# Gate and up products of two SwiGLU blocks: one product of 512 columns for high and low activations, a bank per output half

## What is computed

```python
def swiglu(x, w_gate, w_up, w_down):
    return (jax.nn.silu(x @ w_gate) * (x @ w_up)) @ w_down

h = h + 0.5 * swiglu(rms_norm(h, ffn1_norm[i]), ffn1_w_gate[i], ffn1_w_up[i], ffn1_w_down[i])
...   # sparse attention, retention, merge, output projection
h = h + 0.5 * swiglu(rms_norm(h, ffn2_norm[i]), ffn2_w_gate[i], ffn2_w_up[i], ffn2_w_down[i])
gate = jax.nn.sigmoid(rms_norm(h, ple_norm[i]) @ w_ple_gate[i])
h = h + gate * (p[i] @ w_ple_proj[i])
```

## Time and profile before

| | us |
|---|---|
| median of 3 runs | 1147.44 (1146.24 to 1151.64) |
| profiled execution | 1146.73 |
| its span, first to last instruction | 1144.9 |
| PE busy | 1097.3 (96%) |
| DVE busy | 707.1 (62%) |
| ACT busy | 516.7 (45%) |
| TensorE share of the chain that ended last | 73% |

### The profile page before, as it was taken

How to read it: one execution, slowest core, us unless ns; L and a number is a source line. 1 busy time by engine, 2 the same in 40 slices (tenths; PEclk the granted TensorE clock), 3 DMA queues, 4 the chain that set the end, 5 groups by cost and what they waited for, 6 DMA issues and landing times.

```text
span 1144.9 us, 19072 instructions
## 1 busy us (share of the span) xinstructions
PE 1097.3 (96%) x7962; PEld 931.6 (81%) x7962; DVE 707.1 (62%) x1129; ACT 516.7 (45%) x803; POOL 0.2 (0%) x4
## 2 busy tenths in 40 slices
PE   5989999899999999999999989999999999999997
PEld 3789888554555554999999978888799999999996
DVE  2889777322332334785865679986656775655667
ACT  3774224111111113754444477377944554443455
POOL 0000000000000000000000000000000000000000
PEclk9999999899999999999999999999999999999998
DMA  9955618999999947365554433443336545445321
GB/s 384 399 198 212 247 50 324 422 421 415 412 404 410 409 190 318 144 236 198 199 196 158 158 111 129 146 139 103 104 139 228 202 170 218 184 161 208 129 92 38
DMA packets 38155, 257.74 MB, mean 225 GB/s; under 512 B 4368, under 2 KB 5264, under 8 KB 7856
## 3 DMA queue, kind: packets, MB, share of 16 engines
q1 hardware_dynamic: 36720, 252.38, 57.6%
q10 hardware_dynamic: 1344, 4.08, 0.9%
HBM read 255.39 MB, written 1.05 MB: 224 GB/s over the span
## 4 chain that ended last, share of the span: by engine, by line
PE 73%; DVE 15%; ACT 6%; issue 3%; DMA 2%; ACTq 0%; DVEq 0%
PE bank L535 72%; DVE wl L1811 4%; ACT wh L1242 2%; DMA early<-in_w_ada 1%; DMA csts<-in_cst 1%; DVE xt L1861 1%; DVE arena L2397 1%; DVE rstd L1835 1%; DVE small L2396 1%; ACT arena L1252 1%; DVE acc L1873 1%; DVE hl L1878 1%; PE bank L921 0%; ACT arena L1590 0%; ACT L1252 0%
## 5 line engine op out<-in xcount | busy, mean ns | idle before, releaser
L535 PE MATMUL bank<-hh,wh 128*128 128x256 f32 (+2 forms) x1256 | 362.8, 289 | 6.1 <-DVE wl L1811 4.3
L535 PE MATMUL bank<-hl,wh 128*128 128x256 f32 (+2 forms) x1256 | 358.3, 285 | 0.0
L535 PE MATMUL bank<-hh,wl 128*128 128x256 f32 (+2 forms) x1256 | 358.3, 285 | 0.0
L1811 DVE TENSOR_TENSOR wl<-raw,wh 128x1024 fp32r<-128x1024 f32 (+4 forms) x238 | 267.6, 1163 | 82.7 <-ACT wh L1242 79.3
L1242 ACT ACTIVATE wh<-raw 128x1024 fp32r<-128x1024 f32 (+4 forms) x238 | 227.8, 1003 | 70.0 <-PE bank L535 69.9
L535 PEld LDWEIGHTS bank<-hh,wh 128*128 128x128 f32 (+1 forms) x1256 | 240.8, 192 | 15.4 <-issue 10.4
L535 PEld LDWEIGHTS bank<-hl,wh 128*128 128x128 f32 (+1 forms) x1256 | 240.9, 192 | 1.1
L535 PEld LDWEIGHTS bank<-hh,wl 128*128 128x128 f32 (+1 forms) x1256 | 240.9, 192 | 1.0
L535 PE MATMUL bank<-yh,wh 128*128 128x256 f32 x512 | 146.8, 287 | 0.5 <-DVE yl L1831 0.5
L535 PE MATMUL bank<-yl,wh 128*128 128x256 f32 x512 | 145.5, 284 | 0.0
L535 PE MATMUL bank<-yh,wl 128*128 128x256 f32 x512 | 145.5, 284 | 0.0
(11 more groups left out here) (279 smaller groups left out, 1392.8 us busy)
## 6 DMA issues: line engine op xcount, KB each, us to landing
raw<-in_gu SPq DMA_DIRECT2D x40, 1024.0 KB, 11.0
arena<-in_gu SPq DMA_DIRECT2D x24, 1024.0 KB, 9.9
raw<-in_gd SPq DMA_DIRECT2D x22, 1024.0 KB, 8.6
raw<-in_w_adt SPq DMA_DIRECT2D x14, 1024.0 KB, 5.6
raw<-in_f1g SPq DMA_DIRECT2D x11, 1024.0 KB, 4.8
raw<-in_f1d SPq DMA_DIRECT2D x11, 1024.0 KB, 5.4
raw<-in_f2g SPq DMA_DIRECT2D x11, 1024.0 KB, 4.8
raw<-in_f2u SPq DMA_DIRECT2D x11, 1024.0 KB, 4.9
```

The costliest lines, as they stand in the source:

```text
L535: return pe.matmul(o, l, m, start=start, stop=stop, skip_group_check=True)
L1811: v.tensor_tensor(WL[slot_of[U]][:, 0:n], src, WH[slot_of[U]][:, 0:n].bitcast(f32), ALU.subtract).then_inc(S("wl"), 1)
```

## The change

- Gate and up weights are laid out anew on the host: a unit is now one output half (128 columns) with all eight input blocks, not both output halves with four input blocks (`halves` in place of `even`).
- `hh` and `hl` become one tensor `hb`, so that high and low activations of one input block can be named as one operand of 2 x 256 columns (`HL0`, `HL1`).
- `lin_wide` replaces `lin_fm` for the gate and up products of f1 and f2: for each output half and input block one product of 512 columns with the high weights (high and low activations side by side in a bank) and one of 256 columns with the low weights into the bank's first half. A product takes a bank for each output half. For the very first gate block, whose input arrives block by block, the halves are interleaved by four input blocks.
- VectorE adds the two halves of a bank (`ffn_sum`, a tensor_reduce over pairs of columns 256 apart) into SBUF, for two gate banks and two up banks a step. The scaling and the product with the up part then read SBUF; the order is gate sums, scale, up sums, scale, wait for SiLU, product, low part.
- The bank plan: f1 step 0 has 4, 0 (gate) and 5, 6 (up), step 1 has 1, 2 and 7, 4, later steps 0, 1 and 2, 3. f2 has 0, 1 and 2, 3 in every step, with 4 for the last of step 0.

The core of the diff:

```diff
-            HHt, HLt = ob("hh", 4096), ob("hl", 4096)
+            HB = ob("hb", 8192)
...
+        HHt, HLt = HB[:, 0:4096], HB[:, 4096:8192]
...
+        HB5 = HB[:, :].rearrange("p (s h k t) -> p s h k t", s=2, h=2, k=8)
+        HL0, HL1 = HB5[:, :, 0], HB5[:, :, 1]
...
-        rot = over([0, 1, 2, 3])
-        job(("f1", "g", 0), 4)
-        job(("f1", "u", 0), 5)
+        by_half = lambda P, i, *banks: fixed_to(banks, *[(P, c, i, m) for c in "gu" for m in range(2)])
+        by_half("f1", 0, 4, 0, 5, 6)
         job("f1a", 3)
-        for i in range(1, 11):
-            rot(("f1", "g", i), ("f1", "u", i))
+        by_half("f1", 1, 1, 2, 7, 4)
+        for i in range(2, 11):
+            by_half("f1", i, 0, 1, 2, 3)
...
-        rot = over([0, 1, 2])
         for i in range(11):
-            rot(("f2", "g", i), ("f2", "u", i))
+            by_half("f2", i, 0, 1, 2, 3 if i else 4)
...
+            def lin_wide(P, c, i, X, ready=None):
+                U = 2 * where[P + c, i]
+                bs, ws = {}, {}
+                for m, x in [(m, 4 * u + k) for u in range(2) for m in range(2) for k in range(4)] if ready else [(m, x) for m in range(2) for x in range(8)]:
+                    if x == 0:
+                        ws[m] = weights(U + m, 8)
+                        bs[m] = take(pe, (P, c, i, m))
+                    if ready and m == 0:
+                        pe.wait_ge(*nth(ready[0], ready[1][x]))
+                    h, l = ws[m]
+                    mm(two(bs[m]), h[:, x, :], X[:, :, x, :], x == 0, False)
+                    t = mm(bs[m][:, 0:256], l[:, x, :], X[:, 0, x, :], False, x == 7)
+                    if x == 7:
+                        t.then_inc(S("used"), 1)
...
-            def ffn_act(i, P, G, T, rs, g, u):
-                done(v, g, i)
+            def ffn_sum(i, P, c, T, m):
+                v.wait_ge(*nth("used", units_used(2 * where[P + c, i] + m)))
+                b = bank((P, c, i, m))
+                return v.tensor_reduce(T[i % 2][:, m, :].unsqueeze(2), b[:, :].rearrange("p (s t) -> p t s", s=2), AX.X, ALU.add)
+
+            def ffn_gate(i, P, G, rs):
                 if i >= 2:
-                    evicted(v, (P, "u", i - 2))
-                v.tensor_tensor(G[i % 2], two(bank((P, "g", i))), rs, ALU.mult).then_inc(copied((P, "g", i)), 1)
-                v.wait_ge(*nth(P + "_s", i + 1))
-                done(v, u, i)
+                    v.wait_ge(*nth(P + "_t", i - 1))
+                ffn_sum(i, P, "g", G, 0).then_inc(copied((P, "g", i, 0)), 1)
+                step(ffn_sum(i, P, "g", G, 1))
+                evicted(v, (P, "g", i, 0))
+                prev()
+                v.tensor_tensor(G[i % 2], G[i % 2], rs, ALU.mult).then_inc(copied((P, "g", i, 1)), 1)
+
+            def ffn_up(i, P, G, T, rs):
                 if i >= 2:
                     v.wait_ge(*nth(P + "_yl", i - 1))
-                v.tensor_tensor(T[i % 2], G[i % 2], two(bank((P, "u", i))), ALU.mult).then_inc(copied((P, "u", i)), 1)
-                evicted(v, (P, "u", i))
-                v.tensor_tensor(T[i % 2], T[i % 2], rs, ALU.mult).then_inc(S(P + "_t"), 1)
+                for m in range(2):
+                    ffn_sum(i, P, "u", T, m).then_inc(copied((P, "u", i, m)), 1)
+                for m in range(2):
+                    evicted(v, (P, "u", i, m))
+                chain(v.tensor_tensor(T[i % 2], T[i % 2], rs, ALU.mult))
+                v.wait_ge(*nth(P + "_s", i + 1))
+                v.tensor_tensor(T[i % 2], T[i % 2], G[i % 2], ALU.mult).then_inc(S(P + "_t"), 1)
+                v.wait_ge(*nth(P + "_t", i + 1))
                 low_act(i, P, T)
...
+    def halves(w):
+
+        K, n = w.shape
+        return np.ascontiguousarray(w.reshape(K // 128, 128, n // 256, 2, 128).transpose(2, 1, 3, 0, 4).reshape(n // 256, 128, 2 * K))
```

## The result

The changed kernel takes 1160.97 us (median of 4 runs, 1158.88 to 1163.70), the kernel before beside it 1148.76 (4 runs, 1146.24 to 1151.64): a ratio of 1.0102, 95% interval 1.0081 to 1.0124. That is 1.0% slower, in the forecast's direction, but about twice the forecast's size, and 1 us above the range of 1149 to 1160. The profiled execution took 1158.88 us with a span of 1157.1, against 1146.73 and 1144.9.

A forecast was written before the change was run, and what follows sets the result against it. TensorE, 96% busy, was taken as the bound. On 1146.73 us: +9.6 (f1's start), -3.4 (rest of f1), +3.4 (f2's start), -4.3 (rest of f2), +1.6 (clock) = +6.9, so 1153.6 us; range 1149 to 1160.

The forecast's parts named there:

- the banks: Starts of f1 and f2: TensorE waits for banks that VectorE frees late, costing +9.6 us and +3.4 us.
- the sums: VectorE's four added bank sums a step: 0.69 us each, 2.7 us a step, costed at nothing in the steady loop.
- The upper bound of 1.22 us: Most that one VectorE sum of a bank was allowed to take; the lower bound was 0.61 us.
- rival B: VectorE becomes the bound: sums take 1.22 us, 2.1 us more per step, about 1159.5 us in all; chance 12%.
- Cover just holds: f1's step 5: despite VectorE's extra jobs, the gate sum comes 1.9 us before TensorE wants its bank back.
- the clock in f2: After 3.8 us idle in f2, one stretch of some 3.4 us at 1.2 GHz was to cost +1.6 us.
- The bounds of 0 and 3.2 us: Lowest and highest cost allowed for the low clock behind f2's idle stretch, around the expected 1.6 us.
- the saving of a pair: Gate and up products of f1 and f2: one 512- and one 256-column product take 0.347 us, saving 13.3 ns.
- they start 0.22 to 0.23 us apart: Spacing of 512-column products elsewhere in the kernel, taken as 0.227 us, against 0.24 for two of 256.
- Rival A: Wide product saves nothing, its operand being two pieces or the fixed part doubling: 7.7 us missing, 1161 us; chance 12%.
- Step 0's up and step 1's gate save 0.43, so step 1's up starts at 478.66: Start of f1: two faster blocks bring step 1's up product and the statistics product 0.43 us earlier.
- rival D: Bank waits as forecast, but the clock falls more often, twice in f1 or longer in f2: 1155 to 1158; chance 15%.

The follow-up runs named there:

- experiment 1: Changed kernel with steps 0 to 2 of f1 and step 0 of f2 in the old form on old banks: 1144.22 us, ratio 0.9943 to the kernel before.
- experiment 2: Also written narrow_f1: changed kernel with only steps 0 to 2 of f1 in the old form, f2 wide throughout: 1149.28 us, ratio 0.9997.
- experiment 3: Changed kernel with only step 0 of f2 in the old form, f1 wide from step 0: 1159.74 us, ratio 1.0075.
- experiment 12: Changed kernel with the old form at both starts, as in experiment 1, and every sum of a bank made twice: 1151.70 us, ratio 1.0018.
- experiment 10: Changed kernel with small unread products meant to fill TensorE's three idle stretches and keep the clock up: 1164.26 us, ratio 1.0124.
- split_product: Changed kernel with every 512-column product made as two of 256 columns, banks and sums kept: 1164.02 us, ratio 1.0141.
- experiment 5: Changed kernel with high and low activations of an input block stored side by side, so the operand is one piece: 1161.81 us, ratio 1.0116.
- experiment 7: The kernel of experiment 1 with eight 512-column products first, then eight of 256, in each output half: 1141.75 us, ratio 0.9929.
- experiment 11: Also written first_split: changed kernel with only f1's very first gate block making its wide product as two of 256 columns: 1160.75 us, ratio 1.0090.

## Why the prediction was half right

**Right: the banks.** Step 1's up product was to idle 8.2 us and did 7.93; step 2's second gate half was to go on at 498.35 and did at 499.46, with TensorE already 0.95 us behind at the statistics product; f2 was to idle 3.8 and idled 3.50. Statistics product to step 3 was predicted as 478.0 to 518.2, 40.2 us, and was 40.58. Experiments 1, 2 and 3 show that these waits go when the banks are not reused, each at its own place.

**Right: the sums.** 0.69 us taken from the earlier trace rows, 685 ns measured for all 88. The upper bound of 1.22 us and with it rival B are out, although the Trainium skill (VectorE: DVE Perf Modes, "Rules for kernel authors") calls tensor_reduce the slowest operation of the engine: here it equals the tensor_tensor of the same input size. "Cover just holds" was right too: in f1's steps 3 to 10 no wait for a sum, with 21% of VectorE's time left; experiment 12 shows that twice the sums would not have fitted there.

**Right in size, not certain: the clock in f2.** 1.6 us predicted from the earlier trace rows, 1.56 and 1.34 measured by experiments 10 and 2. But with the same 3.50 us of idling the clock was low for 3.4 us in the changed kernel, not at all in narrow_f1, and for 6.8 us in first_split and split_product, where it fell 0.8 and 1.5 us before TensorE went on. First_split's last piece took 177.08 us, 2.6 more than narrow_f1's. The bounds of 0 and 3.2 us hold all of these.

**Wrong in size: the saving of a pair.** The step that failed is "they start 0.22 to 0.23 us apart": I took 0.227 from a stretch of the first block in which products of 512 columns follow each other. In f1 and f2 a wide product is followed by a narrow one after 0.237 us, and a pair saves 6.7 ns instead of 13.3. Over 576 pairs that is 3.8 us that were not given back, 1.7 in f1 and 2.1 in f2; the table's rows for the rest of f1 and of f2 are short by 1.6 and 1.8. Rival A had named the term and was right by half. Its first reason was not: experiment 5 rules out the two-piece operand. Experiment 7 gives half of it to the alternation of sizes, for 0.231 + 0.119 us. The other half stands in the first products of each group; why they are slower stays open. By the Trainium skill (TensorE: Matmul & The Clock Gate, "Back-to-back issue gap") a pair would save 2.5 ns; the measured 6.7 lies between its rule and my row, and nearer to the rule.

**Missed: the wait ahead of step 0's up product.** The second step that failed is "Step 0's up and step 1's gate save 0.43, so step 1's up starts at 478.66": it lets step 0's up product start when it did before, and has the clock at full speed behind it. The up product starts 8.79 us after f1's first product, 8.13 before, and TensorE idles 2.42 us ahead of it instead of 1.64. Behind that the clock fell to 0.50 for 3.4 us. The statistics product came 1.96 us later instead of 0.43 earlier. Of these 2.4 us, 0.66 are the later start (8.79 - 8.13) and 1.7 the clock (1.56) with the half-sized saving of two blocks (0.2).

The faster block alone doesn't make the longer idle stretch: its last product starts just 0.14 us earlier (6.08 against 6.22 us after the first). The rest of the 0.78 us is the later start. What TensorE waits for is not the weight split that the trace names before:

```profile
466.82 0.36 PE L535 MATMUL bank<-hh,wh 128*128 128x256 f32 x1 [1.64 <-DVE wl L1811]
```

That split (465.22 to 466.45) had ended 0.37 us earlier, in the changed kernel 1.25 us earlier. The first gate block is the end of a branch in TensorE's program, and the DMA records show transfers of instructions here. Queue 8 in two stretches of 5 us, 461.7 to 466.7 before and 460.3 to 465.3 after (packets, MB, share of 16 engines):

```profile
q8 instruction: 2, 0.03, 2.9%
```

```profile
q8 instruction: 2, 0.03, 4.3%
```

Queue 8 made 66 of these 16 KB transfers for 7962 products before and 60 for 7258 after, 121 products each, so I take it for TensorE's. The two transfers start 3.79 and 5.18 us after f1's first product before, 4.58 and 5.00 after, and both are over at 6.49 and 7.11. In all fourteen traces TensorE goes on 1.46 to 1.71 us after that: the nine kernels with a narrow first block have the transfers at 6.35 to 6.70, the five with a wide one at 6.98 to 7.43. So the wait fits one for instructions behind the branch, and these came later. Why they come later behind a wide block no run shows.

Experiment 11 shows that the first block sets it off: that block slowed again, nothing else, the low clock gone, 2.2 us back. The other traces agree: in the five kernels with a wide first block the idle stretch here is 2.18 to 2.45 us and the clock falls behind it, in the nine with a narrow one (the kernel before among them) it is 1.51 to 1.82 and it doesn't.

**The sum again.** Predicted +6.9, measured +12.2 in the profiled executions. The 5.3 us between them: start of f1 2.7, rest of f1 1.6, start of f2 0.2, rest of f2 1.8, and -1.0 in the stages that the change doesn't touch.

**The range.** Rival A at 1161 and rival D at 1155 to 1158 were weighed as cases that exclude each other, next to a forecast with each term at its best value. They are terms of one sum: half of A and a low stretch as in D, with the later start ahead of it, came together, 3.8 + 2.4 us, and lead from 1153.6 to 1159.8. A range of independent terms has to take in two of them going wrong the same way. The chances of a slower kernel (0.60) were on the right side, and would have been larger.

## What to carry to other kernels

When an operand takes more banks, list for each bank its last reader's time and its next writer's time at the start of the stage, not in the steady loop, and do it again for the plan that repairs it: here the gain of 3.9 us in 576 pairs was paid back three times over by three waits, 12.8 us, and moving one wait off a bank made a longer one on another. If only the first steps are short of banks, give only these the old form: that turned 1.0% slower into 0.6% faster (0.7% with products of one size in a row). A product made faster ahead of a wait gives nothing; look at what the wait is for, since here it got longer and the clock fell behind it.

## What the hardware showed that I had not expected

- A product's distance to the next depends on its neighbours: 512 columns take 0.227 us in the earlier trace rows and 0.237 in turns with 256 columns; in groups of eight 0.235 to 0.239 for the first two and 0.227 for the last three, even for the very last, which 256 columns follow. 256 columns take 0.116 in turns with wide ones, 0.119 to 0.12 among themselves.
- A moving operand in two pieces 4096 columns apart streams like one in one piece (0.237 and 0.116 us both ways).
- The granted clock fell behind all five idle stretches of 2.18 to 2.45 us ahead of f1's first up product and behind none of the nine of 1.51 to 1.82 us there. But ahead of f2's step 1 the same 3.50 us gave a low stretch of 0, 3.4 or 6.8 us, for 0, 1.3 to 1.6 and 2.6 us of time.
- TensorE stood still 1.46 to 1.71 us beyond the end of two 16 KB instruction transfers behind a branch, in all fourteen traces. The idle time reads "issue" in some and names a weight split, already done, in others.
